# Three edits to a hybrid mLSTM, convolution and expert layer: one-hots split over two engines, expert sums over eight units, and an interleaved start

## The reference

```python
q = (t @ w_query).reshape(T, PEER_HEADS, 2, PEER_HALF)
s = jnp.einsum('thpk,pnk->thpn', q, sub_keys)
s_val, s_idx = lax.top_k(s, PEER_TOPK)
cand = s_val[..., 0, :, None] + s_val[..., 1, None, :]
best, pos = lax.top_k(cand.reshape(T, PEER_HEADS, 256), PEER_TOPK)
expert = ...                       # 8 heads x 16 experts a token
gate = jax.nn.softmax(best, -1)
act = gelu(einsum('td,ted->te', t, u_emb[expert])) * gate
out = einsum('te,ted->td', act, v_emb[expert])
```

## Time and profile before

| | |
|---|---|
| time before | 3449.22 us, median of 3 runs (3443.9 to 3451.1) |
| profiled execution | 3447.79 us, its span 3446.0 us |
| PE matmul busy | 3373.8 us, 98% of the span, 16931 matmuls |
| DVE, ACT, POOL busy | 2367.3 us (69%), 1008.6 us (29%), 1805.6 us (52%) |
| TensorE clock granted | 0.99 of full speed over the span |
| DMA | 874.72 MB, mean 254 GB/s |

### The profile page before, as it was taken

The page is one execution under the profiler, slowest core; times in us unless marked ns, Lnnn a source line. Parts: engine busy times, 40 slices in busy tenths (PEclk is TensorE's granted clock), DMA queues, the critical chain, the costliest instruction groups (busy, mean ns, idle before and its releaser), DMA issues.

```text
span 3446.0 us, 44792 instructions
## 1 busy us (share of the span) xinstructions
PE 3373.8 (98%) x16931; PEld 2935.1 (85%) x16931; DVE 2367.3 (69%) x3856; ACT 1008.6 (29%) x1152; POOL 1805.6 (52%) x904
## 2 busy tenths in 40 slices
PE   6999999999999999999999999999999999999998
PEld 3688888766888899999999999999888888888886
DVE  2288886746414759993887798864667776767766
ACT  3332211244123232223222222223233233323233
POOL 1210000213444345676666666666777777778764
PEclk8999999999999999999999999999999999999999
DMA  9655643565423236776677767778988888888872
GB/s 371 257 190 201 220 155 120 184 230 205 161 98 147 90 125 244 265 289 268 266 304 300 290 270 310 307 306 321 377 321 333 318 322 330 316 321 329 320 275 98
DMA packets 184619, 874.72 MB, mean 254 GB/s; under 512 B 16621, under 2 KB 77501, under 8 KB 97844
## 3 DMA queue, kind: packets, MB, share of 16 engines
q1 hardware_dynamic: 122160, 525.38, 41.9%
q0 software_dynamic: 38688, 281.15, 20.2%
q10 hardware_dynamic: 23652, 66.69, 5.1%
HBM read 803.78 MB, written 69.32 MB: 253 GB/s over the span
## 4 chain that ended last, share of the span: by engine, by line
PE 88%; DVE 7%; DMA 2%; POOL 1%; issue 1%; ACT 1%; ACTq 0%; DVEq 0%; SPq 0%; POOLq 0%
PE bank L2096 82%; PE bank L2357 2%; PE bank L2473 1%; DMA ring<-in_w_mod 1%; PE bank L2331 1%; DVE b L1861 1%; POOL low L770 1%; DVE rows_a L1800 1%; DMA low<-in_conv_w 1%; DVE b L1841 0%; PE bank L2104 0%; DVE rows_c L1800 0%; PE bank L2457 0%; DVE tiny L1856 0%; DVE rows_b L1800 0%
## 5 line engine op out<-in xcount | busy, mean ns | idle before, releaser
L812 POOL TENSOR_TENSOR split<-ring,split 128x1024 fp32r<-128x1024 f32 x544 | 1303.6, 2410 | 542.6 <-ACT split L1150 540.4
L2096 PE MATMUL bank<-h_hi,split 128*128 128x384 f32 (+1 forms) x4608 | 1222.0, 341 | 8.2 <-POOL split L812 7.0
L1150 ACT ACTIVATE split<-ring 128x1024 fp32r<-128x1024 f32 x544 | 578.0, 1063 | 1607.0 <-PE bank L2096 1584.9
L2096 PE MATMUL bank<-split,a_split 128*128 128x512 f32 x4608 | 1045.0, 389 | 0.1
L2096 PEld LDWEIGHTS bank<-split,a_split 128*128 128x128 f32 x4608 | 865.0, 188 | 179.8 <-POOL split L812 0.5
L2096 PEld LDWEIGHTS bank<-h_hi,split 128*128 128x128 f32 x4608 | 839.4, 188 | 29.6 <-POOL split L812 8.8
L2096 PE MATMUL bank<-h_lo,split 128*128 128x384 f32 (+1 forms) x2304 | 785.2, 341 | 0.0
L1978 DVE TENSOR_TENSOR acc<-acc,bank 128x512 f32<-128x512 f32 x372 | 251.6, 683 | 289.7 <-PE bank L2096 288.8
L2096 PEld LDWEIGHTS bank<-h_lo,split 128*128 128x128 f32 x2304 | 433.8, 188 | 9.4
L2096 PE MATMUL bank<-hT_hi,w_hi 128*128 128x512 f32 (+1 forms) x768 | 289.8, 377 | 5.4 <-POOL ring_lo L732 2.2
L2096 PE MATMUL bank<-hT_lo,w_hi 128*128 128x512 f32 (+1 forms) x768 | 287.1, 374 | 0.0
(11 more groups left out here) (317 smaller groups left out, 3789.9 us busy)
## 6 DMA issues: line engine op xcount, KB each, us to landing
ring<-in_u_emb SPq DMA_DIRECT2D x128, 1024.0 KB
ring<-in_v_emb SPq DMA_DIRECT2D x128, 1024.0 KB
ring<-in_w_mod SPq DMA_DIRECT2D x48, 1024.0 KB
ring<-in_w_in SPq DMA_DIRECT2D x44, 1024.0 KB
ring<-in_w_mod SPq DMA_DIRECT2D x64, 512.0 KB, 4.5
neurons<-tiny ACTq DMA_DIRECT2D x128, 192.0 KB
gate_table<-b ACTq DMA_DIRECT2D x6, 4096.0 KB, 14.8
weigh<-neurons SPq DMA_DIRECT2D x32, 768.0 KB
```

The costliest lines, as they stand in the source:

```text
L812: nc.gpsimd.tensor_tensor(split[:, r % 2, 1, at].bitcast(F32R), ring[:, r % 4, :, :].rearrange("p k n -> p (k n)")[:, at], split[:, r % 2, ...
L1150: nc.scalar.activation(split[:, q % 2, 0, at].bitcast(F32R), ring[:, q, :, :].rearrange("p k n -> p (k n)")[:, at], ACT.Copy)\
L2096: last = mm(out_, left[a].bitcast(F32R), right[b].bitcast(F32R), start=start and n == 0, stop=stop and n == 2)
```

## The change

It has three parts that act, and some bookkeeping.

1. *One-hots.* The plain plane (0) of each group is made by ScalarE as 1 - |iota - index| cut at zero, with four Abs and one Relu, a unit ahead of its use. It stands ahead of the two weight halves of a unit. ScalarE's chunk loop becomes straight code for this. TensorE waits for `rows_made` too.
2. *Sums in eights.* Two groups share a PSUM sum: the units of an eight alternate between the two groups, and each pair of units is one quarter of the columns, added into `acc` once. The turn-over to the next two groups is spread: products in units 5 and 6, copies on ScalarE in the middle of units 6 and 7, rests on VectorE at the head of units 7 and 0. Rows are not added in unit 7.
3. *Beginning.* Row quarters 4, 5, 6 and 7 come behind x tiles 0 and 1, 2, none, and 3.

Six semaphores are folded into others, and two small tiles (`h2_last`, `nval_last`) move. Its core:

```diff
@@ SyncE
+            def v_load(unit, group, k):
                 sp.wait_ge(split_made, unit * 2 + 2 * (V0 - 3))
...
-                    if k == 2 and not first:
-                        sp.wait_ge(a_split_made, i * 2)
-                        weigh_load(i * 2 + 1, 1)
-                    if k == 6 and not last:
-                        sp.wait_ge(a_split_made, i * 2 + 1)
-                        weigh_load(i * 2 + 2, 0)
-                    v_load(i * 8 + k, i * 2 + k // 4, k % 4)
+                    if k in (2, 4) and not last:
+                        sp.wait_ge(a_split_made, i * 2 + k // 2)
+                        weigh_load(i * 2 + 1 + k // 2, k // 2 - 1)
+                    v_load(i * 8 + k, i * 2 + k % 2, k)
@@ ScalarE
+            def onehot_rows(grp):
+
+                act.wait_ge(slotT_made, 2)
+                act.wait_ge(onehot_used, grp + 1)
+                rows = onehot[:, grp % 2, :, 0, :]
+                for s in range(4):
+                    last = nc.scalar.activation(rows[:, s, :].bitcast(F32R), iota, ACT.Abs,
+                                                bias=expT[:, 1, 4 * grp + s:4 * grp + s + 1])
+                last.then_inc(row_step, 1)
+                act.wait_ge(row_step, grp + 1)
+                nc.scalar.activation(rows.bitcast(F32R), rows, ACT.Relu, bias=one_col, scale=-1.0)\
+                    .then_inc(rows_made, 1)
...
+                ahead = GROUPS_AT[(k + 1) % CHUNK_UNITS] if unit + 1 < PRE + CHUNKS * CHUNK_UNITS else 0
+                for h in range(2):
+                    if h < ahead:
+                        onehot_rows(group)
+                        group += 1
+                    next_hi(unit, unit % 4, h)
+                finish_neurons(unit, unit % 4)
...
-            def sweep_unit(unit, q):
-                for h in range(2):
-                    next_hi(unit + NK, q, h)
+            def sweep_unit(unit, q, turn=None):
+                next_hi(unit + NK, q, 0)
+                if turn:
+                    act.wait_ge(split_used, (unit + NK) * 2 + (2 * U0 + 2))
+                    a_hi(*turn)
+                next_hi(unit + NK, q, 1)
...
-                    sweep_unit(i * 8 + k, k % 4)
-                    if k % 4 == 1:
-                        a_hi((k // 4 + 1) % 2, i * 2 + (k // 4 + 1))
+                    sweep_unit(i * 8 + k, k % 4, (k - 6, i * 2 + (k - 4)) if k > 5 else None)
@@ VectorE
-                    nc.vector.tensor_scalar(onehot[:, grp % 2, s, 0, :].bitcast(F32R), iota_bank, expT[:, 1, tok],
-                                            None, ALU.is_equal)
...
+            def flush_here(unit, j):
+                if unit % 2:
+                    (merge if unit >= NK - 8 else flush)(unit // 2, j)
+
             weigh_group(0)
             dot(NK - 5)
             rest_group(0)
+            weigh_group(1)
             dot(NK - 4)
+            rest_group(1)
             rows_added = 0
             for unit in range(NK):
-                g = unit // 4
-                flush_here = merge if g == GROUPS - 1 else flush
+                g, k = unit // 8 * 2, unit % 8
+                if k == 7 and g + 2 < GROUPS:
+                    rest_group(g + 2)
+                if k == 0 and g:
+                    rest_group(g + 1)
                 flush_here(unit, 0)
-                if unit % 4 == 0 and g + 1 < GROUPS:
-                    weigh_group(g + 1)
+                if k in (5, 6) and g + 2 < GROUPS:
+                    weigh_group(g + k - 3)
...
                 flush_here(unit, 1)
-                if unit % 4 == 2 and g + 1 < GROUPS:
-                    rest_group(g + 1)
-                while rows_added < SLOTS and 3 + rows_added - rows_added // 8 <= unit:
+                while k < 7 and rows_added < SLOTS and 3 + rows_added - rows_added // 8 <= unit:
                     add_rows(rows_added)
@@ TensorE
-                    for t in range(LT):
-                        for g in range(4):
-                            turn_x(t, g)
+                for t in ((0, 1), (2,), (), (3,))[n - 4] if 4 <= n < 8 else ():
+                    for g in range(4):
+                        turn_x(t, g)
                 pe.wait_ge(quarter_full[q], 16 * (i + 1))
                 row_quarter(4 + i % 2, q, q)
...
                 pe.wait_ge(onehot_made, count)
+                pe.wait_ge(rows_made, count)
...
+            def sums(i, k, first=False):
+
+                unit, s = i * 8 + k, k % 2
+                pe.wait_ge(a_split_made, i * 2 + (s + 1))
                 for j in range(JD):
-                    o = JD * k + j
+                    o = JD * (k // 2) + j
...
-                    elif not first or o > 3:
-                        pe.wait_ge(sum_free, unit * JD + (j - 3))
+                    elif s == 0 and (not first or o > 3):
+                        pe.wait_ge(sum_free, i * (4 * JD) + (o - 3))
```

More of the change, by code:

```diff
@@ L294, in hybrid_layer @@
         act_s = small[:, 1792:1920]
+        h2_last = small[:, 1920:2048]
+        nval_last = tiny[:, 2720:2848]
         ga2_part = [small[:, i * NB:(i + 1) * NB] for i in range(3)] + [ga2_last]
@@ L440, in hybrid_layer @@
         onehot_made = sem("onehot_made")
+        row_step = sem("row_step")
+        rows_made = sem("rows_made")
         onehot_used = sem("onehot_used")
@@ L655, in weigh_load, with sweep_loads @@
                   .then_inc(weigh_full[s], 16)
-            def sweep_loads(i, first=False, last=False):
+            def sweep_loads(i, last=False):
                 for k in range(8):
@@ L1267, in neurons, with finish_neurons @@
                     next_hi(unit, q, h)
+                finish_neurons(unit, q, store, wait)
+            def finish_neurons(unit, q, store=True, wait=True):
                 if store:
@@ L1289, in _ @@
                     nc.scalar.activation(expT[:, q - 1, :] if q < 3 else gate_rest,
-                                         bank[:, 6 + (q - 1) % 2, 0:TD], ACT.Copy)\
+                                         bank[:, 6 + (q - 1) % 2, 0:TD], ACT.Copy, scale=-1.0 if q == 2 else 1.0)\
                         .then_inc(slotT_made, 1)
@@ L1294, in _ @@
             act.sem_inc(table_stored, 16)
-            with act.Fori(0, CHUNKS) as chunk:
-                for k in range(CHUNK_UNITS):
-                    neurons(chunk * CHUNK_UNITS + (PRE + k), k % 4)
-                act.wait_ge(gbank_free, chunk * 16 + (1 + 16))
-                act.dma_start(gate_dram[bass.ds(chunk, 1), :, :, :].rearrange("a p i t -> p (a i t)"),
-                              stage.rearrange("p i t -> p (i t)")).then_inc(table_stored, 16)
+            def onehot_rows(grp):
[9 more added lines that the diff above has]
+                    .then_inc(rows_made, 1)
+            group = 0
+            for _ in range(GROUPS_AT[0]):
+                onehot_rows(group)
+                group += 1
+            for unit in range(PRE, PRE + CHUNKS * CHUNK_UNITS):
+                k, chunk = (unit - PRE) % CHUNK_UNITS, (unit - PRE) // CHUNK_UNITS
+                ahead = GROUPS_AT[(k + 1) % CHUNK_UNITS] if unit + 1 < PRE + CHUNKS * CHUNK_UNITS else 0
+                for h in range(2):
+                    if h < ahead:
+                        onehot_rows(group)
+                        group += 1
+                    next_hi(unit, unit % 4, h)
+                finish_neurons(unit, unit % 4)
+                if k == CHUNK_UNITS - 1:
+                    act.wait_ge(gbank_free, 1 + 16 * (chunk + 1))
+                    act.dma_start(gate_dram[chunk, :, :, :].rearrange("p i t -> p (i t)"),
+                                  stage.rearrange("p i t -> p (i t)")).then_inc(table_stored, 16)
             def a_hi(s, group):
```

113 lines of the change are left out of this document (50 added, 63 removed).

## The result

The changed kernel takes 3467.78 us, median of 6 executions (3464.26 to 3473.44), where the kernel before takes 3449.43 beside it (3443.88 to 3451.1). The ratio is 1.0055 with an interval of 1.0044 to 1.0066: slower by 0.55%, 18 us. The forecast was 3453, its range 3439 to 3462. The result lies outside.

The account below looks back on a forecast made before the run. TensorE, busy 98% of the span, was taken to bound the kernel, and DMA its beginning. Terms -5.8 + 0 + 12.9 - 3.1 = +4.0 gave 3451.8 us on the profiled execution, 3453 as median; range 3439 to 3462.

Parts of the forecast that it names:

- start: Beginning: row quarters between x tiles close the DMA gap from 35 to 45 us; -5.8 us, ends 0 and -6.5.
- one-hots: One-hot stage: Abs and Relu work moved to ScalarE hides in its waits for TensorE; 0, ends 0 and +5.
- turn-overs: Sweep: late row delays gather and weight rest at six of fourteen turn-overs, 2.15 us each; +12.9, ends 0 and +20.
- SyncE's loads: Sweep: v loads behind the wait for a_split at k = 2 land in 10 to 12 us, hidden; 0.
- tail: Behind TensorE's last matmul: VectorE has no backlog and ends at E + 9.5 instead of E + 12.6; -3.1 us.
- Rival 3: Beginning: the start does not carry its saving, since TensorE could bind before DMA from 45 to 108; 3459, chance 0.06.
- Rival 2: Sweep: SyncE's held load is late at every turn-over, +14 on top of the stalls; 3467, chance 0.17 with its milder form.
- Rival 1: Sweep: the turn-overs stay hidden and the two savings stand alone; -8.9, 3440, chance 0.27.
- rival 4: One-hot stage: Relu needs a table load, making ScalarE late in 2-group units; 3453 to 3513, chance 0.03.

Follow-up runs that it names:

- run 16: The changed kernel, unchanged, measured again on another chip: 3464.25 us, ratio 1.006 to the kernel before.
- runs 5: The kernel before with only row quarters 4 to 7 put between the turned x tiles: 3440.69 us, one execution.
- run 14: The changed kernel with run 4's edits and rows 31 and 95 added one unit earlier: 3443.78 us, ratio 0.9995 to the kernel before.
- run 15: The changed kernel with run 14's edits, but all x tiles turned ahead of row quarter 4 as before: 3444.18 us, ratio 0.9999 to the kernel before.
- runs 6 and 7: The kernel before with first_piece making one of three matmuls, the second also with row quarters between x tiles: 3449.87 and 3447.49 us, one execution each.
- Run 2: The changed kernel with the first eight's held weigh loads issued behind its v loads: 3461.15 us, ratio 1.0032 to the kernel before.
- run 4: The changed kernel with rows also in unit 7, first weigh loads behind the v loads, later held loads at k = 4 and 6: 3449.24 us, ratio 0.9999.
- Run 1: The changed kernel with gathered rows added in unit 7 too: 3459.73 us, ratio 1.0024 to the kernel before.
- run 8: The changed kernel with the row left out in unit 7 added at unit 8's head, ahead of VectorE's rest: 3461.08 us, one execution.

## Why the prediction was wrong

Term by term, forecast and measured on the two profiled executions: start -5.8 and +0.8; one-hots 0 and 0; turn-overs +12.9 and +14.8; SyncE's loads 0 and +6.8; tail -3.1 and -3.3. The sum was +4.0, it is +19.1. Two steps failed, by 6.6 and 6.8 us in these executions. The size of the first is the less certain: the changed kernel's sweep started 6.4 us earlier in run 16. Taken from the medians instead, less the sweep and the tail of the profiles, the start term is +0.2 us at first and -1.5 in run 16 (estimates), so most of the 5.8 is missing there too. Run 16's sweep is 1068.4 us, 23.3 over the kernel before, so the loss in the sweep does not hang on one execution.

- **"DMA gains 5.8 ... I take -5.8."** The transfer gap closed as said: 10 us at 350 instead of 130 GB/s are worth 5.2 us at 420. But from 45 to 108 the rate fell from 420 to 392, 4.2 us' worth over 63 us. The step that failed is that the earlier transfers are kept: "TensorE then has quarters 8 to 11 three to five us earlier", with "the stretch up to 108 is set by DMA as before". That stretch carried less than before, and it did so in two ways. In the changed kernel's own profile the share of the queues stays near 1 and TensorE is not full, while the rate is lower. Windows before and after:

```profile
60.00:75.00 15.00, 14.66 (x84) 8.80 (x83) 0.17 (x1) 1.17 (x2) 4.58 (x1) 1.00 1.01 418
60.00:75.00 15.00, 14.47 (x88) 7.59 (x86) 2.03 (x6) 1.75 (x3) 3.04 (x1) 1.00 0.97 362
```

No run shows why the queues moved less there. In runs 5 and 14 the share itself fell (0.78 and 0.77) where TensorE had no idle time, at clocks of 0.85 and 0.84. Rival 3 had this form: it read from the earlier trace rows, TensorE busy 57 of 63 us, that TensorE could bind before DMA; I gave that 0.06. The low clock does not need the new start: run 15, with the old one, has 0.79 there, a share of 0.92, and its next stage begins at 136.11. That TensorE is the cause is argued, and it fits only the second form; runs 6 and 7 did not settle it. The cause stays open.
- **"SyncE's loads ... Hidden; 0."** The 0 was worked out for the load held at k = 2 of an ordinary eight, and there it held at all turn-overs but the first: behind unit 15 the v load was issued at 2520.69 and there at 2531.92. At unit 10 it took from 2453.66 to 2469.57, 15.9 us where 10 to 12 were reckoned, and TensorE waited 0.73 and 0.69 us. The first eight units had no term at all. There the `weigh` loads stand ahead of the v loads of units 4 and 6 and share the queues with the three `x_dense` tiles, which the 3.7 to 4.7 MB of the burst leave out; the load took 20.5 us, TensorE stood 2.93 us, and the clock was 0.79 from 2420 to 2428. Run 2 gives 4.3 of the 6.8 back, and with the held loads of run 4 no such wait is left. Rival 2 had the mechanism, but at every turn-over. That its 3467 is what was measured is luck: it summed six stalls and fourteen late loads, where the runs show six stalls, two late loads and a start that gained nothing.
- **The turn-overs** came as worked out, at the six places named and with the times named. At unit 71 the row runs from T8 + 3.3 to T8 + 5.6 (2991.22 to 2993.57), the gather goes at T8 + 5.9 (2993.84), the rest runs to T8 + 11.6 (2999.53). Two waits of 1.18 and 0.66 were forecast as 1.1 and 1.0; a pair costs 2.47, not 2.15, since the pieces behind the waits are each 0.3 us longer than their matmuls at the sweep's rate (1.67 us for six, where 1.36 was reckoned). Two of the forecast's sums are off in the last place (11.65 - 8.16 - 1.36 is 2.13, and 24.5 less 1.06 and 2.4 is 21.0); nothing hangs on them. Rival 1 is refuted. Run 1 shows the row as the cause, and that putting it back is not free: VectorE's rest took 1.75 us where GpSimd made no subtraction, and up to 6.44 beside two.
- **One-hots and tail** were right. 384 Abs of 0.389 and 96 Relu of 0.725 us, 191 us in all where 200 was reckoned, hide in ScalarE's waits for TensorE, with no change in the matmul count. ScalarE's table loads from 1500 to 2380 are two in both kernels, so Relu needed none (rival 4), as the Trainium skill's page on activation tables, "ScalarE: Activation LUTs", Table sets, has it.

## What to carry to other kernels

When a gap in the transfers is closed, look whether the next stretch can keep the gain before it is put into a sum: here that stretch was full already, its TensorE was busy nine tenths of it, and most of the 5.8 us did not arrive. When a wait is put into a transfer queue, work out the burst behind it separately for the first round, with every queue that loads in it. When a deferred step shares an engine with a gather's release, follow what is queued behind that gather; and count units with a double load separately, since they were the ones at which the obvious repair failed. Before a profiled execution is taken as the size of an effect of a few us, profile the same kernel again: here two profiles of one kernel differed by 6.4 us ahead of the sweep.

## What the runs showed that was not expected

- VectorE's subtraction of 1536 columns took 1.75 us alone and up to 6.44 beside GpSimd's subtractions; its mean went from 1871 ns before to 2825 in the changed kernel and 3624 in run 14, and in these two TensorE never waited for it.
- An indirect DMA's issue on GpSimd took 2.20 us while that subtraction ran, where it took 0.94 in the changed kernel (2993.84) beside a row addition.
- Waits of TensorE of like length were followed by a lower clock in one execution and not in another: 2.60 us in run 8 by 0.83 over ten us, 2.54 in run 4 by 1.00. Ahead of the sweep the same wait of 3.40 us near 858 was followed by 58 matmuls in 14.52 us in the changed kernel's first profile and in 12.83 in run 16. That is 1.7 of the 6.4 us between the two.
